# How the first microseconds of a two-block transformer kernel are fed: input in pieces, other order of the first products

## The reference

```python
h = jnp.concatenate([meta, x], axis=1)             # 16 + 256 = 272 tokens, 1024 wide
hn = rms_norm(h, g_mix[0])                         # h * g * rsqrt(mean(h*h) + eps)
z = hn @ w_in                                      # first product: 1024 x 2216
c_q, c_kv, k_pe, fq, fk, fv, f_logit = jnp.split(z, ...)
```

## Time and profile before

| | |
|---|---|
| time, median of 3 runs | 1388.16 us (1387.38 to 1391.67) |
| the profiled execution's own time | 1393.52 us |
| its span, first to last instruction | 1391.6 us |
| PE busy | 1334.9 us, 96% of the span |
| DVE, ACT, POOL busy | 966.0, 736.4, 462.4 us |
| mean granted TensorE clock | 0.978 of full speed |
| moved by DMA | 230.53 MB, mean 166 GB/s |

### The profile page before, as it was taken

One profiled execution on the slowest core, in us unless ns is written; L12 is line 12 of the kernel. 1 busy time (PEld: TensorE's weight loads), 2 busy tenths in 40 slices (PEclk: granted clock), 3 DMA queues, 4 the chain that ended last, 5 costly groups with the idle time before them and its releaser, 6 DMA issues.

```text
span 1391.6 us, 29208 instructions
## 1 busy us (share of the span) xinstructions
PE 1334.9 (96%) x10776; PEld 1298.5 (93%) x10776; DVE 966.0 (69%) x1446; ACT 736.4 (53%) x1224; POOL 462.4 (33%) x492
## 2 busy tenths in 40 slices
PE   5999999999999999999999999999999969999997
PEld 5787699999999999999989999999998859999996
DVE  6767567664477677555655679997578786999844
ACT  5454645444444454444545456665446844766642
POOL 3532044321111443211636324333126563333310
PEclk9998999999999999999999999999999969999998
DMA  7440045555555555555525545554554426455451
GB/s 268 150 149 32 1 152 174 186 185 184 180 181 183 180 180 183 190 187 186 195 92 183 187 175 185 183 182 169 189 202 162 137 94 223 159 191 189 143 203 53
DMA packets 34508, 230.53 MB, mean 166 GB/s; under 512 B 3838, under 2 KB 4990, under 8 KB 10662
## 3 DMA queue, kind: packets, MB, share of 16 engines
q1 hardware_dynamic: 33652, 226.47, 46.8%
q10 hardware_dynamic: 770, 2.90, 0.6%
HBM read 228.17 MB, written 1.05 MB: 165 GB/s over the span
## 4 chain that ended last, share of the span: by engine, by line
PE 77%; issue 8%; DVE 6%; ACT 4%; POOL 4%; DMA 1%; POOLq 0%; DVEq 0%; ACTq 0%; SPq 0%
PE ps L378 25%; PE ps L379 25%; PE ps L380 25%; DVE wlo L343 2%; POOL xlo L468 2%; ACT whi L338 2%; POOL ssum L474 1%; PE ps L1085 1%; DMA raw<-w 1%; DVE rstd L442 1%; DVE work L1470 1%; POOL q_mla L1857 1%; DVE work L1441 0%; PE ps L422 0%; ACT work L1752 0%
## 5 line engine op out<-in xcount | busy, mean ns | idle before, releaser
L343 DVE TENSOR_TENSOR wlo<-raw,whi 128x1024 fp32r<-128x1024 f32 (+1 forms) x448 | 546.5, 1225 | 106.2 <-ACT whi L338 105.2
L378 PE MATMUL ps<-xhi,whi 128*128 128x256 f32 (+2 forms) x2064 | 586.5, 284 | 18.5 <-DVE wlo L343 13.9
L379 PE MATMUL ps<-xlo,whi 128*128 128x256 f32 (+2 forms) x2064 | 584.6, 283 | 0.0
L380 PE MATMUL ps<-xhi,wlo 128*128 128x256 f32 (+2 forms) x2064 | 583.5, 283 | 0.0
L338 ACT ACTIVATE whi<-raw 128x1024 fp32r<-128x1024 f32 (+1 forms) x448 | 448.5, 1008 | 141.2 <-PE ps L380 136.9
L378 PEld LDWEIGHTS ps<-xhi,whi 128*128 128x128 f32 x2064 | 391.9, 190 | 23.2 <-issue 15.9
L380 PEld LDWEIGHTS ps<-xhi,wlo 128*128 128x128 f32 x2064 | 392.3, 190 | 0.0
L379 PEld LDWEIGHTS ps<-xlo,whi 128*128 128x128 f32 x2064 | 389.9, 189 | 0.3
L378 PE MATMUL ps<-hhi,whi 128*128 128x256 f32 (+1 forms) x1184 | 338.0, 285 | 7.7 <-POOL hlo L1947 7.4
L380 PE MATMUL ps<-hhi,wlo 128*128 128x256 f32 (+1 forms) x1184 | 335.7, 283 | 0.0
L379 PE MATMUL ps<-hlo,whi 128*128 128x256 f32 (+1 forms) x1184 | 335.5, 283 | 0.0
(11 more groups left out here) (262 smaller groups left out, 1314.3 us busy)
## 6 DMA issues: line engine op xcount, KB each, us to landing
raw<-w SPq DMA_DIRECT2D x184, 1024.0 KB, 4.9
raw<-w SPq DMA_DIRECT2D x40, 768.0 KB, 4.2
h<-x_fm ACTq DMA_DIRECT2D x1, 1088.0 KB, 6.4
out_fm<-h SPq DMA_DIRECT2D x8, 128.0 KB, 2.0
ws<-ws_src ACTq DMA_DIRECT2D x1, 512.0 KB, 5.0
bs<-bs_rows ACTq DMA_DIRECT2D x1, 512.0 KB, 5.8
consts<-constants ACTq DMA_DIRECT2D x1, 508.0 KB, 9.7
q_fox<-decay_rows SPq DMA_DIRECT2D x1, 340.0 KB
```

Source lines behind the costliest of these rows:

```text
L343: nc.vector.tensor_tensor(wlo[:, j % HLR, 0:n], raw[:, slot, col:col + n], whi[:, j % HLR, 0:n].bitcast(F32), ALU.subtract).then_inc(wlo_d ...
L378: nc.tensor.matmul(o, hi, xh, start=start, stop=False)
L379: nc.tensor.matmul(o, hi, xl, start=False, stop=False)
L380: mm = nc.tensor.matmul(o, lo, xh, start=False, stop=stop)
```

## The change

- x comes in four DMAs of two kt each, all from ACT's queue, each with its own semaphore.
- The first slab comes in two DMAs of one unit each. The parameters come in two: the first 88 columns ahead of the slabs, the other 520 columns behind the padding rows. DVE waits for these before it uses `lam`, late in the program.
- Four buffers instead of two hold the gained x (`gained`: two of `xg`, two of `tmp`).
- `xlo` of the even kt stays on POOL; that of the odd kt goes to DVE (L1198 of the changed kernel).
- The squares are summed by POOL instead of DVE.
- Units 0 and 1 are ordered by kind of product (`first_unit`): eight products of high parts, then eight with low x, then eight with low weights, each with its own waits.
- `pe_stats` moves from behind unit 1 to behind unit 2, ACT's root to behind tile 2, DVE's reciprocal and its reading of tile 0 from tile 0's place to tile 3's, and the first steps of the forget gate from tile 1's place to tile 3's.
- PE begins with 18 products of a zeroed tile (256 columns) into a bank that is not otherwise used then, as soon as DVE has cleared that tile. PE waits for the constants only before `pe_stats`.

The diff (context cut):

```diff
 LA = 3
+WARM = 18
...
         rows_loaded = sem("rows_loaded")
-        x_loaded = sem("x_loaded")
+        x_loaded = [sem(f"x_loaded{i}") for i in range(4)]
+        xlo_odd = sem("xlo_odd")
         raw_full = [sem(f"raw_full{i}") for i in range(RAW)]
...
         raw_tiles = [*range(TL_FQ, TL_FV)] + [*range(TL_KN, TL_V)]
+        gained = [xg[:, 0, :], xg[:, 1, :], tmp[:, 0, :], tmp[:, 1, :]]
         latent_tiles = [*range(TL_CKV, TL_KN)]
...
         def _(sp):
-            sp.dma_start(params[:, :], params_in).then_inc(small_in, 16)
+            first = pcol["conv_w"][0]
+            sp.dma_start(params[:, 0:first], params_in[:, 0:first]).then_inc(small_in, 16)
...
                 if rnd0 == 0:
-                    body(0, wait=False)
+                    half = UB * P
+                    sp.dma_start(raw[:, 0, 0:half], src[0][:, 0:half]).then_inc(s("unit0_loaded"), 16)
+                    sp.dma_start(raw[:, 0, half:cols], src[0][:, half:cols]).then_inc(raw_full[0], 16)
+                    for k in range(1, RAW):
+                        sp.dma_start(raw[:, k, 0:cols], src[k]).then_inc(raw_full[k], 16)
...
                     sp.dma_start(k_fox[64:FOX_K, :, :], pad_in[1]).then_inc(pad_done, 16)
+                    rest = pcol["conv_w"][0]
+                    sp.dma_start(params[:, rest:npar], params_in[:, rest:npar]).then_inc(s("params_loaded"), 16)
                     with sp.Fori(1, n) as i:
...
             p = ph["attn_in"]
-            pe.wait_ge(consts_in_done, 16)
+            pe.wait_ge(s("warm_set"), 1)
+            for _ in range(WARM):
+                nc.tensor.matmul(ps[:, 7, 0:SEQ], chi[:, 0, 0:P], chi[:, 0, 0:SEQ], start=True, stop=True)
             t = [0]
...
                 bank = take()
-                need = (lambda b: pe.wait_ge(xlo_done, b + 1)) if u == 0 else None
                 mm = unit(pe, u // UB, u % UB, [(ps[:, bank, 0:T0], b == 0, b == 7) for b in range(8)],
-                          [x_rhs(b, 0, T0) for b in range(8)], need)
+                          [x_rhs(b, 0, T0) for b in range(8)])
                 mm.then_inc(unit_done, 1)
-                if u == 1:
-                    pe_stats(pe, 0, 0, T0)
...
+            def first_unit(u):
...
+                bank = take()
+                o = ps[:, bank, 0:T0]
+                pe.wait_ge(whi_done, u + 1)
+                for b in range(8):
+                    if u == 0:
+                        pe.wait_ge(xhi_done, b + 1)
+                    nc.tensor.matmul(o, whi[:, u, b * P:(b + 1) * P], xhi[:, b, :], start=b == 0, stop=False)
+                for b in range(8):
+                    if u == 0 and b % 2:
+                        pe.wait_ge(xlo_odd, (b + 1) // 2)
+                    elif u == 0:
+                        pe.wait_ge(xlo_done, b + 2)
+                    nc.tensor.matmul(o, whi[:, u, b * P:(b + 1) * P], xlo[:, b, :], start=False, stop=False)
+                pe.wait_ge(wlo_done, u + 1)
+                for b in range(8):
+                    mm = nc.tensor.matmul(o, wlo[:, u, b * P:(b + 1) * P], xhi[:, b, :], start=False, stop=b == 7)
+                mm.then_inc(unit_done, 1)
...
             for u in range(0, U_KN):
-                whole(u)
+                if u < 2:
+                    first_unit(u)
+                else:
+                    whole(u)
+                if u == 2:
+                    pe.wait_ge(consts_in_done, 16)
+                    pe_stats(pe, 0, 0, T0)
                 if u in (5, 9):
...
         def _(dve):
+            nc.vector.memset(chi[:, 0, :].bitcast(F32), 0.0).then_inc(s("warm_set"), 1)
             dve.wait_ge(small_in, 16)
-            dve.wait_ge(x_loaded, 16)
-            for kt in range(KT):
-                dve_gain(dve, 0, kt, kt % 2, 0, T0)
-                if kt == 4:
-                    split_lo(dve, 0, 0, 8)
-            for j in range(1, LA):
-                split_lo(dve, 0, j, 8)
-            for kt in range(KT):
-                dve.wait_ge(sq_done, kt + 1)
-                dve.wait_ge(ssum_done, kt + 1)
-                nc.vector.tensor_tensor(ssum[:, :], ssum[:, :], sq[:, kt % 2, :], ALU.add).then_inc(ssum_done, 1)
...
+            def first_gain(kt):
+                dve.wait_ge(x_loaded[kt // 2], 16)
+                if kt >= 4 and kt % 2 == 0:
+                    dve.wait_ge(xlo_done, kt - 2)
+                elif kt >= 4:
+                    dve.wait_ge(xlo_odd, (kt - 3) // 2)
+                nc.vector.tensor_scalar(gained[kt % 4], h[:, kt, :], par(NORM_GAIN[0], kt), None,
+                                        ALU.mult).then_inc(xg_done, 1)
...
+            def first_xlo(kt):
+                dve.wait_ge(xhi_done, kt + 1)
+                nc.vector.tensor_tensor(xlo[:, kt, :], gained[kt % 4], xhi[:, kt, :].bitcast(F32),
+                                        ALU.subtract).then_inc(xlo_odd, 1)
+            for kt in range(4):
+                first_gain(kt)
+            first_xlo(1)
+            first_gain(4)
+            first_gain(5)
+            first_xlo(3)
+            split_lo(dve, 0, 0, 8)
+            first_gain(6)
+            first_gain(7)
+            first_xlo(5)
+            split_lo(dve, 0, 1, 8)
+            first_xlo(7)
             nc.vector.memset(soft[:, :, :, :], 1.0).then_inc(s("soft_set"), 1)
             nc.vector.memset(q_inv[:, :, :], 1.0).then_inc(s("soft_set"), 2)
+            split_lo(dve, 0, 2, 8)
             split_lo(dve, 0, LA, 8)
-            dve_rstd(dve, 0, 0, T0)
...
                     inverse(2)
-                if t in dve_tiles:
+                if t in dve_tiles and t:
                     ready, n = tile_ready(t)
                     dve.wait_ge(ready, n)
-                if t == 0:
...
+                if t == 3:
...
+                    dve_rstd(dve, 0, 0, T0)
+                    dve.wait_ge(unit_done, 1)
+                    src = ps[:, 0, 0:T0]
                     nc.vector.tensor_tensor(logit, src[0:8, :], rstd[0:8, :], ALU.mult).then_inc(s("logit"), 1)
...
                                                        in1=sin4, op0=ALU.mult, op1=ALU.mult).then_inc(tile_free, 1)
-                if t == 1:
+                if t == 3:
                     c = s("fg_step")
...
+            dve.wait_ge(s("params_loaded"), 16)
             for _ in dve_log_sigmoid(dve, par("lam", 0, NB), log_lam[:, :], tmp[:, 0, 0:NB], tmp[:, 1, 0:NB],
...
         def _(act):
-            act.dma_start(h[:, :, :], x_in).then_inc(x_loaded, 16)
+            for i in range(4):
+                act.dma_start(h[:, 2 * i:2 * i + 2, :], x_in[:, 2 * i:2 * i + 2, :]).then_inc(x_loaded[i], 16)
             act.dma_start(consts[:, :], consts_in).then_inc(consts_in_done, 16)
             act.dma_start(sel_in, rows_in).then_inc(rows_loaded, 16)
...
+            def first_xhi(kt):
+                act.wait_ge(xg_done, kt + 1)
+                nc.scalar.activation(xhi[:, kt, :], gained[kt % 4], ACT.Copy).then_inc(xhi_done, 1)
             for kt in range(KT):
-                act_xhi(act, 0, kt, kt % 2, 0, T0)
-                if kt in (2, 4, 6):
-                    split_hi(act, 0, kt // 2 - 1, 8, first=True)
+                first_xhi(kt)
+                if kt == 3:
+                    act.wait_ge(s("unit0_loaded"), 16)
+                    nc.scalar.activation(whi[:, 0, :], raw[:, 0, 0:UB * P], ACT.Copy).then_inc(whi_done, 1)
+                if kt in (5, 7):
+                    split_hi(act, 0, (kt - 3) // 2, 8, first=True)
             for kt in range(KT):
                 act_square(act, 0, kt, kt % 2, 0, T0)
-            split_hi(act, 0, LA, 8, first=True)
-            act_root(act, 0, 0, T0)
+                if kt == 3:
+                    split_hi(act, 0, LA, 8, first=True)
...
                     nc.scalar.activation(q_sq[:, t - TL_Q, :], src, ACT.Square).then_inc(n_sq[3], 1)
+                if t == 2:
+                    act_root(act, 0, 0, T0)
                 if t == 4:
...
             nc.gpsimd.memset(four[:, :], 4.0).then_inc(four_set, 1)
+            for kt in range(0, KT, 2):
+                pool.wait_ge(xhi_done, kt + 1)
+                nc.gpsimd.tensor_tensor(xlo[:, kt, :], gained[kt % 4], xhi[:, kt, :].bitcast(F32),
+                                        ALU.subtract).then_inc(xlo_done, 2)
             for kt in range(KT):
-                pool_xlo(pool, 0, kt, kt % 2, 0, T0)
+                pool_ssum(pool, 0, kt, kt % 2, 0, T0)
             pool.wait_ge(rows_loaded, 16)
```

## The result

| | before | changed |
|---|---|---|
| median | 1388.78 us (1384.97 to 1393.82, 20 runs) | 1392.68 us (1388.62 to 1398.23, 20 runs) |
| profiled execution, its span | 1393.52, 1391.6 us | 1393.32, 1391.6 us |
| PE, POOL busy | 1334.9, 462.4 us | 1337.4, 468.8 us |

The two profiled spans are equal, and mislead: up to 670 us the changed kernel's trace runs 2.1 us behind (second root at 207.83 against 205.66 us, fifth at 669.73 against 667.58), and then before's trace alone has a stretch of low clock, 6.8 us long from 713.5 us. Whatever the change does is done at the start.

A forecast was written before the change was run, and what follows sets the result against it. The body was taken as bound by PE's matmuls, which the change leaves alone. Unit 4 earlier (-1.3) plus the clock's fall (+1.7) gave +0.4 us on 1388.16, so 1388.6 us, range 1384.5 to 1391.5.

The forecast's parts named there:

- which wait: Ahead of unit 4, PE stands 4.0 us until DVE has read tile 0; no wait for the sums.
- the clock's part: Behind the stand before unit 4 the clock falls and products run slow for 3.5 to 4.2 us: +1.7 us.
- the transfers: At the start, queues take turns by packets, so x's quarters land at 5.3, 7.2, 9.2 and 12.3 us.
- (a): Rival on the start's transfers: x is not held back, landing at 7.3 us as before; 1385.4 us, chance 0.19.
- (c): Slower rival: SP's queue is served ahead of ACT's, x's fourth quarter lands at 17 us; 1393.3 us, chance 0.09.
- The whole chain now starts when unit 2 ends: Before unit 4: from unit 2's end, root, reciprocal and reading of tile 0 take 7.65 us.
- the sums done at 22.8 us: POOL's eight sums of squares end between 21.8 and 23.9 us, taken as 22.8, costing PE no wait.
- the 30.85 forecast: Unit 4 starts at 23.2 + 7.65 = 30.85 us, 1.3 us earlier than before.
- Unit 2 ends at 23.2 us: On PE, with the pace fast from 17.0 us, 5.9 us ahead of before; 22.4 to 24.5 us possible.
- I put the same difference on the median: The +0.4 us against before's profiled execution was added to before's median of 1388.16 us.
- rival (b): The clock stays up at the start, or tile 0 is not late, with x as before: 1383.5 us, chance 0.11.

The follow-up runs named there:

- e3: Changed kernel with 38 zero products of 256 columns behind unit 3, filling PE's stand before unit 4: median 1390.75 us, ratio to before 1.0017.
- e9: Changed kernel with the eight sums of squares on DVE again instead of POOL: median 1391.21 us against 1389.5 for before, ratio 1.0011.
- e6: Kernel before with 18 zero products of 256 columns ahead of `pe_stats`, filling its 2.0 us stand: median 1389.49 us against 1387.87, ratio 1.001.
- e1: The bank experiment: changed kernel with tile 0 in bank 5 instead of bank 0: median 1388.24 us against 1387.65 for before, ratio 1.0003.
- e7: Kernel before with only x in four transfers and the first slab in two: median 1388.97 us, ratio to before 1.0012.
- e8: Changed kernel with tile 0 in bank 5 and x in one transfer, slab still in two: median 1387.65 us against 1387.87 for before, ratio 0.9995.
- e4: Changed kernel without the 18 zero products at the start: median 1393.63 us, ratio to before 1.0036.
- e10: Changed kernel with tile 0 in bank 5, x in one transfer and the sums on DVE: median 1386.78 us against 1389.5 for before, ratio 0.998.

## Why the prediction was wrong

- **Right: which wait.** Units 0 to 2 do end sooner (24.84 against 29.1 us), PE hardly waits for the sums any more (0.3 us in the second trace), and what stands ahead of unit 4 is tile 0, released by DVE's L1287, with the clock falling behind it. The bank experiment shows that without this wait there is no loss; the fill puts the clock's part at 1.5 us in one trace (1.7 forecast).
- **Right: the transfers.** The queues do take turns: from 7 to 8 us 73 packets against 70, from 10 to 11 us 53 against 54. The last quarter was gained at 12.44 us (12.3 forecast). The first came at 3.92 instead of 5.3 us, which helped nobody, since PE waited for the first high weights until 9.35. Rivals (a) and (c) are out.
- **Failed: "The whole chain now starts when unit 2 ends", with the sums done at 22.8 us.** It started at ACT's last square, which waited for POOL's sums. In the changed kernel's two traces and in e3 the statistics begin at 24.84, 24.59 and 24.59 us, and the root at 27.43 in all three; in seven traces with the sums on POOL the root comes 4.8 us after the last square. The sums ended at 24.44 us (22.8 forecast, 23.9 at most). They began at 15.50 instead of 15.0 us, a single add with its hand-over took 0.91 instead of 0.85 us, and the two that ran beside DVE's low weights cost 1.8 us more, where 1.0 was counted for such collisions. So the root began at 27.43 us where 25.2 was forecast: 2.2 us. Behind it, from root to unit 4, the chain took 5.45 us (5.64 forecast), so unit 4 began 2.0 us later than the 30.85 forecast, at 32.88.
- **Failed as well, and hidden behind the sums: "Unit 2 ends at 23.2 us".** It ended at 24.84, past my upper end of 24.5. I let the pace turn fast at 17.0 us, from the 3.5 to 4.2 us of two restarts in before's trace. It turned at 19.7, 6.4 us after 13.32. In those 2.7 us PE makes at the slow pace 2.7 / 0.227 = 12 products instead of 21: 1.2 us. The other 0.4 us is the last low part of x, which was POOL's (kt 6): it took 2.13 us, to 15.54 us, where DVE's was forecast as the last at 15.2. In e9, with no sums on POOL, the root comes 2.2 us after unit 2's end. From that I estimate that the late unit 2 alone would have put the root at 26.4 to 27.0 us in the changed kernel's traces. Mending the sums alone could not have given the forecast's 25.2.
- **Failed: the base.** "I put the same difference on the median" took the fall of the clock at 24 us in the one trace of before for a part of the kernel. It is there in two traces of three, and the mean mark for unit 4 is 34.71 us, not 35.35. The base is 0.6 us off by this, from three traces; e6, which fills that stand, shows no gain in the median.
- Together, by the reading of unit 4's tile: forecast +0.4 against before's first trace; 2.0 us later than that in the changed kernel's first (37.72 for 35.75), 0.5 for the mean with its second, which runs slow for all of unit 4, 0.6 for the base: +3.5, where the medians differ by 3.9.
- **The range.** By the terms named for its upper end (unit 2 at 24.5: 1.3 us more, a whole slow unit 4: 0.7 more) it would end at 1390.6; the 1391.5 given has 0.9 us that no term pays for. The measured 1392.68 lies above both. By its own -4.4 rival (b) gives 1383.8, not 1383.5.
- **Rival (b)**, a clock held up, was wrong too: the 18 zero products bring nothing that shows. The slower rival (c) had its mechanism in the wrong place. What came is the forecast's own wait, with the sums and unit 2 both past their upper ends.

What stays open: e1 spreads `inv` 1.7 us earlier than before does on average and is not faster, and e6 and e7, which leave the marks up to the spread where they are, have medians 0.1% above before's with intervals that reach 1. From the spread to the second root before takes 156.0 to 156.9 us, e1 157.5 and e8 158.8, with 13.7 and 16.6 us at the low clock in that stretch, against 10.2 to 13.7 in before's three traces; what sets those falls I have not found. That x whole is better than x cut rests on root and spread alone: the intervals of e1 and e8 overlap.

## What to carry to other kernels

Starting PE earlier is worth nothing when the next thing it needs comes off a chain on other engines: put the links of that chain (sums, root, reciprocal, the reading that frees a bank) first, and ask of each moved step which buffer it frees and who wants that next. Here a spare bank for one tile took back the whole loss, while the transfers in pieces, alone, gave nothing that shows. When two chains meet, look at what the engine between them was doing: ACT had no gap for 4.8 us before the root, so an earlier end of unit 2 would not have moved that root. And before a difference of a few us is put on a median, look whether the trace it starts from holds stretches of low clock that another execution might not have.

## What was not expected of the hardware

- A stand of 2.0 us took the granted clock down in two executions of the same kernel and not in a third; stands of 2.5 to 4.6 us did in each of the five traces that have one ahead of unit 4. Behind the stands of 1.6 to 1.8 us ahead of the spread it fell in five traces of eleven.
- From where PE began to work without long gaps at the start to the fast pace it took 6.4 us in the changed kernel's first trace, 5.5 in e4 and 3.1 in e10, and 3.5 us from the restart at 24 us in before.
- An add of 128x272 on POOL took 0.77 us, as a subtraction of that shape did alone (0.76), with 0.14 us to the next; beside DVE's low weights it took 1.57 and 1.76 us, and DVE was slower too (1.47 and 1.74 us instead of the 1.22 of other low weights). Eight adds with two such meetings came to 8.94 us.
- Matmuls of zeros held the clock in e3: 38 of them kept it at 1.00 over 4.7 us.
